# A fused encoder layer on one core: value projections first from unscaled x, weight sums one up turn earlier, two down steps prepared

## The reference, cut to what matters

```python
h = rms_norm(x, norm_mix)                       # x: (512 tokens, 1024)
q_a, k_a, v_a, q_b, k_b, v_b, u_c, g = split(h @ w_in)
o_a = chunked_rel_attention(q_a, k_a, v_a, q_norm_a, k_norm_a, rel_bias_a)   # 8 heads x 64
o_b = stick_breaking_attention(q_b, k_b, v_b)                                # 8 heads x 64
o_c = multiscale_pool(u_c, w_pool, pool_scale)
merged = sig(g0) * (o_a @ w_branch_a) + sig(g1) * (o_b @ w_branch_b) + sig(g2) * (o_c @ w_branch_c)
x = x + merged @ w_out
h2 = rms_norm(x, norm_ffn)
x = x + (silu(conv(h2 @ w_up_gate)) * conv(h2 @ w_up_value)) @ w_down        # conv of width 3 over tokens
```

## Time and profile before

| what | value |
|---|---|
| median of 3 runs | 835.34 us (834.24 to 835.59) |
| profiled execution, its own time | 834.84 us |
| its span in the trace | 832.7 us |
| PE busy | 815.1 us, 98% of the span |
| DVE busy | 601.5 us, 72% |
| ACT busy | 402.6 us, 48% |
| DMA | 113.25 MB, mean 136 GB/s |

### The profile page before, as it was taken

How to read it: one execution, slowest core, us unless ns; L and a number is a source line. 1 busy time by engine, 2 the same in 40 slices (tenths; PEclk the granted TensorE clock), 3 DMA queues, 4 the chain that set the end, 5 groups by cost and what they waited for, 6 DMA issues and landing times.

```text
span 832.7 us, 11778 instructions
## 1 busy us (share of the span) xinstructions
PE 815.1 (98%) x3855; PEld 677.1 (81%) x3855; DVE 601.5 (72%) x847; ACT 402.6 (48%) x560; POOL 102.1 (12%) x87
## 2 busy tenths in 40 slices
PE   5999999999999999999999999999999999899998
PEld 4888888888888888888888887888888888688886
DVE  5535888867678676555552579888778789998798
ACT  6434776665546544434341463433333334455653
POOL 2100010000000060000000013332232333300000
PEclk9999999999999999999999999999999999999999
DMA  6333242222222222333363326666556655666455
GB/s 207 103 102 89 66 124 77 79 74 66 86 76 66 74 77 88 93 98 100 89 214 104 129 72 202 203 202 201 189 191 199 196 191 185 218 210 191 149 186 177
DMA packets 129964, 113.25 MB, mean 136 GB/s; under 512 B 6052, under 2 KB 109192, under 8 KB 128528
## 3 DMA queue, kind: packets, MB, share of 16 engines
q1 hardware_dynamic: 129264, 110.77, 42.6%
q0 software_dynamic: 672, 2.12, 0.9%
HBM read 99.21 MB, written 13.65 MB: 136 GB/s over the span
## 4 chain that ended last, share of the span: by engine, by line
PE 93%; DVE 4%; ACT 1%; DMA 1%; issue 1%; SPq 0%; DVEq 0%; ACTq 0%
PE ps L1422 29%; PE ps L1423 28%; PE ps L1424 28%; PE ps L1516 2%; PE ps L1506 2%; PE ps L1531 1%; PE ps L1530 1%; DVE w_lo L872 1%; DMA x_in<-in_x_dram 1%; DVE conv_out L1259 1%; DVE out_sb L1412 0%; DVE conv_out L1262 0%; PE ps L1447 0%; DVE conv_in L1268 0%; ACT w_hi L497 0%
## 5 line engine op out<-in xcount | busy, mean ns | idle before, releaser
L1422 PE MATMUL ps<-h_lo,w_hi 128*128 128x512 f32 x704 | 276.9, 393 | 1.5 <-DVE h_lo L897 0.9
L1423 PE MATMUL ps<-h_hi,w_hi 128*128 128x512 f32 x704 | 274.2, 389 | 0.0
L1424 PE MATMUL ps<-h_hi,w_lo 128*128 128x512 f32 x704 | 274.1, 389 | 0.0
L872 DVE TENSOR_TENSOR w_lo<-w_raw,w_hi 128x1024 fp32r<-128x1024 f32 x119 | 149.8, 1259 | 137.3 <-ACT w_hi L503 77.9
L503 ACT ACTIVATE w_hi<-w_raw 128x1024 fp32r<-128x1024 f32 x97 | 102.8, 1060 | 191.9 <-PE ps L1424 183.4
L1422 PEld LDWEIGHTS ps<-h_lo,w_hi 128*128 128x128 f32 x704 | 132.2, 188 | 29.8 <-issue 1.6
L1424 PEld LDWEIGHTS ps<-h_hi,w_lo 128*128 128x128 f32 x704 | 132.2, 188 | 27.6
L1423 PEld LDWEIGHTS ps<-h_hi,w_hi 128*128 128x128 f32 x704 | 132.2, 188 | 26.5
L481 POOL TENSOR_TENSOR sg<-sg,conv_out 128x512 f32<-128x512 f32 x22 | 37.4, 1700 | 319.2 <-ACT sg L801 319.2
L1262 DVE SCALAR_TENSOR_TENSOR conv_out<-conv_in,par,conv_out 128x512 f32<-128x512 f32 x44 | 50.2, 1141 | 5.5 <-DVE conv_out L1259 0.2
L497 ACT ACTIVATE w_hi<-w_raw 128x1024 fp32r<-128x1024 f32 x23 | 24.4, 1059 | 53.3 <-PE ps L1424 53.2
(11 more groups left out here) (219 smaller groups left out, 1304.7 us busy)
## 6 DMA issues: line engine op xcount, KB each, us to landing
w_raw<-in_w_in_dram SPq DMA_DIRECT2D x104, 256.0 KB, 3.1
w_raw<-in_w_up_dram SPq DMA_DIRECT2D x88, 256.0 KB, 3.2
raw_t<-in_w_down_dram SPq DMA_DIRECT2D x11, 1024.0 KB, 9.1
down_sums<-t_sum SPq DMA_DIRECT2D x11, 1024.0 KB, 5.6
w_raw<-in_w_down_dram SPq DMA_DIRECT2D x33, 256.0 KB, 3.0
w_raw<-down_sums SPq DMA_DIRECT2D x33, 256.0 KB, 3.8
w_raw<-in_w_out_dram SPq DMA_DIRECT2D x16, 256.0 KB, 2.9
w_raw<-down_sums SPq DMA_DIRECT2D x22, 128.0 KB, 2.9
```

Source lines behind the costliest of these rows:

```text
L872: v.tensor_tensor(w_lo[:, slot, :], w_raw[:, slot, :], r32(w_hi[:, slot, :]), ALU.subtract)\
L1422: mm3(dst, l_hi, r_lo, start=start, stop=False, **kw)
L1423: mm3(dst, l_hi, r_hi, start=False, stop=False, **kw)
L1424: return mm3(dst, l_lo, r_hi, start=False, stop=stop, **kw)
```

## The change

Six edits.

1. **Start.** PE transposes x itself, without waiting for r. ACT and DVE split the transposed x (`xt_hi`, `xt_lo`), and the value units of branch A are computed from it first. The gain of norm_mix is multiplied into the value weights (`values_hi`, `values_lo`, the latter two operations of 128x512). r per token is multiplied into the values as they leave PSUM. Meanwhile h is made: DVE adds the parts back (`parts_added`), PE spreads r over a bank with two matmuls (`d_r_hi`, `d_r_lo`), DVE multiplies (`h_sum`), and both engines split again. The order of units becomes four of v_a, one of v_b, q and k of the first heads, and the other three of v_b. Only the first value unit is computed token block by token block.
2. 24 matmuls of 128x128 on constants (`WARM`) stand ahead of everything on PE. SP issues the first value unit after the first block of x. `g_row` is loaded from ACT's queue, and POOL no longer splits a weight unit.
3. **Weight sums.** Pairs 0 and 1 are summed during the w_out stage (after `lo` of its units 3 and 5), pair p in up turn p-1 after that; the last turn has none.
4. **Two steps.** `s_x` and `a_lo_x` of step 1 now stand ahead of the last up turn as well, and behind it only the two weight units of step 1 follow.
5. **Seam.** The last block of `x1` is added in two halves, with its own waits; the order of the transposes is adapted; in the first up turn a split moves ahead of a pair of taps and `spread_r` moves before the end of the second tile.
6. **Last bank.** The last output block is added in two halves of 128x256, stored by SP and by ACT.

```diff
@@ start, ACT
+            xt_split_hi(0)
+            values_hi(N_VA, 0)
+            for t in range(1, TT):
+                xt_split_hi(t)
+            values_hi(N_VA + 1, 1)
+            square(0)
+            square(1)
+            values_hi(N_VA + 2, 2)
...
+            hi(N_QK0 + 1, 0)
+            proj_a(0, 0, QK0_BANK, N_QK0 + 1, False)
+            values_hi(N_VB + 1, 1)
+            proj_a(1, 1, QK0_BANK + 1, N_QK0 + 2, False)
+            values_hi(N_VB + 2, 2)
+            norms_a(0, SS0_BANK)
+            values_hi(N_VB + 3, 3)
+            hat_hi(0, 0)
+            hat_hi(1, 1)
@@ start, SP
+            x_load(0)
+            values(N_VA, 0, V_A * P)
+            for t in range(1, TT):
+                x_load(t)
+            values(N_VA + 1, 1, V_A * P)
+            values(N_VA + 2, 2, V_A * P)
@@ start, PE
+            pe.wait_ge(heads_step, 2)
+            for _ in range(WARM):
+                mm3(ps[:, 2, 0:P], ones_heads[:, :], ones_heads[:, :], start=True, stop=True)
...
+            for t in range(3):
+                x_transposes(t)
+            pe.wait_ge(lo_ready, N_VA + 1)
+            for t in range(TT):
+                pe.wait_ge(xt_lo_ready, t + 1)
+                for kk in range(2):
+                    last = value_product(V_A_BANKS[t], kk, t, slice(kk * WB, kk * WB + WB), 0)
+                if t == 0:
+                    x_transposes(3)
...
+            values(N_VB + 1, V_B_BANKS, 1)
+            sumsq(0, 0, SS0_BANK)
+            sumsq(1, 1, SS0_BANK + 1)
+            values(N_VB + 2, V_B_BANKS, 2)
+            values(N_VB + 3, V_B_BANKS, 3)
@@ w_out stage, DVE
             for u in range(2, KD):
                 lo(N_OUT + u, u % 2)
+                if u in (3, 5):
+                    sums_first((u - 3) // 2)
+                    sums_second((u - 3) // 2)
@@ up, DVE
+                        if isinstance(jj, int) and jj == NP - 1:
+                            continue
                         if (i, gv) == (0, 1):
-                            sums_first(jj)
+                            sums_first(jj + 1)
                         if (i, gv) == (1, 0):
-                            sums_second(jj)
+                            sums_second(jj + 1)
@@ up_first, DVE
-                sums_first(0)
-                sums_second(0)
@@ last up turn, DVE
-            s_x(0, 0)
-            a_lo_x(0, 0)
+            for step in range(2):
+                s_x(step, step)
+                a_lo_x(step, step)
             up(KF // 2 - 1)
-            prepare_x(1, 1)
+            for u in range(2):
+                down_lo(2 + u, 1, u)
@@ end
-            for i, (b8, bank) in enumerate(((0, 4), (2, 5), (1, 6), (3, 7), (4, 0), (6, 1))):
+            for i, (b8, bank) in enumerate(((0, 4), (2, 5), (1, 6), (3, 7), (4, 0))):
...
+            d.wait_ge(bank_done, 6)
+            for q in range(2):
+                o = slice(q * HT, q * HT + HT)
+                v.tensor_tensor(out_sb[:, 6, o], ps[:, 1, o], x1[:, 3, o], ALU.add).then_inc(out_ready, 1)
```

More of the change, by code:

```diff
@@ L41 @@
 Q_A, K_A, V_A, Q_B, K_B, V_B, U_C, GATE = 0, 4, 8, 12, 16, 20, 24, 28
-N_QK0 = 0
-N_VA = 2
+N_VA = 0
+N_VB0 = 4
+N_QK0 = 5
 N_VB = 6
@@ L515, in _, with xt_split_hi, values_hi @@
[L515 to L521, removed]
+            def xt_split_hi(t):
+                a.wait_ge(xt_done, t + 1)
+                act(xt_hi[:, :, t * P:t * P + P], x_turned(t), ACT.Copy).then_inc(xt_hi_ready, 1)
+            def values_hi(n, u):
+                a.wait_ge(w_landed[u % 2], (n // 2 + 1) * 32)
+                if n == 0:
+                    a.wait_ge(gmix_ready, 1)
+                if n >= 2:
+                    a.wait_ge(unit_done, n - 1)
+                for i in range(2):
+                    c = slice(i * WB, i * WB + WB)
+                    last = act(w_hi[:, u % 2, c], w_raw[:, u % 2, c], ACT.Copy, scale=g_mix[:, 2 * u + i:2 * u + i + 1])
+                last.then_inc(hi_ready, 1)
@@ L523, in after, with h_split_hi @@
+            def h_split_hi(k):
+                a.wait_ge(h_sum_ready, k + 2)
+                act(h_hi[:, k:k + 2, :], h_sum[:, k:k + 2, :], ACT.Copy).then_inc(h_hi_ready, 2)
+            h_split_hi(0)
+            h_split_hi(2)
+            hi(N_QK0, 1)
+            for t in range(TT):
+                last = act(v_a[:, t, :], ps[:, V_A_BANKS[t], :], ACT.Copy, scale=tok[:, 5, t:t + 1])
+            last.then_inc(v_stored, 1)
+            h_split_hi(4)
+            h_split_hi(6)
             def after(n):
@@ L792, in up @@
                             down_hi(gv, 0, gv, 0)
-                        elif not (first and e == 0):
+                        elif not (first and e in (0, 2)):
                             hi_at(n + gv + 2, gv, jj * 2 + (N_UP // 2 + i + 1))
@@ new lines, in values_lo @@
+            def values_lo(n, u):
+                d.wait_ge(hi_ready, n + 1)
+                for i in range(2):
+                    c = slice(i * WB, i * WB + WB)
+                    last = v.scalar_tensor_tensor(out=w_lo[:, u % 2, c], in0=w_raw[:, u % 2, c],
+                                                  scalar=g_mix[:, 2 * u + i:2 * u + i + 1], in1=r32(w_hi[:, u % 2, c]),
+                                                  op0=ALU.mult, op1=ALU.subtract)
+                last.then_inc(lo_ready, 1)
@@ new lines, in parts_added @@
+            def parts_added(k):
+                v.tensor_tensor(h_sum[:, k:k + 2, :], r32(xt_hi[:, k:k + 2, :]), r32(xt_lo[:, k:k + 2, :]), ALU.add)\
+                    .then_inc(h_sum_step, 1)
+            d.wait_ge(gmix_ready, 1)
+            xt_split_lo(0)
+            values_lo(N_VA, 0)
+            for t in range(1, TT):
+                xt_split_lo(t)
+            values_lo(N_VA + 1, 1)
+            d.wait_ge(xt_lo_ready, TT)
+            parts_added(0)
+            values_lo(N_VA + 2, 2)
```

326 lines of the change are left out of this document (191 added, 135 removed).

## The result

| what | before | after |
|---|---|---|
| median of 13 runs, same chip | 835.24 us (834.13 to 836.24; one run took 1029.7) | 837.2 us (837.0 to 838.55) |
| ratio | | 1.003, 95% interval 1.0023 to 1.0037 |
| profiled execution, its own time | 834.84 us | 838.45 us |
| its span | 832.7 us | 836.8 us |
| PE busy | 815.1 us | 822.7 us (98%) |

The change makes the kernel slower by 2.0 us. My range ended at 837.2; the likeliest case, "same", was wrong, and what happened is rival (b).

A forecast was written before the change was run, and what follows sets the result against it. PE was taken as the bound, fed except in a few waits, so late units cost their lateness. Terms -2.2 +3.6 +1.7 -0.5 +2.9 -3.5 -1.7 -0.1 gave +0.2: 835.0 us, range 832.5 to 837.2.

The forecast's parts named there:

- "same": Whole kernel: no clear change, neither under 833.7 us nor over 837.0; chance 0.55.
- rival (b): Pauses at the last v_b unit and last up turn's third tile both cost the clock: +1.9, 836.9 us; chance 0.14.
- start, first unit done: Kernel start: the first value unit finishes earlier because PE needs no r, -2.2 us net.
- pause behind `sumsq`: Before the last v_b unit: PE waits for its weight split, queued behind the norms, +3.6 us.
- clock behind it: Slow products after a pause: +1.7 us behind `sumsq`, 0 behind the third tile of turn 10.
- sums out of turn 0: Up turn 1: the late unit at 511.59 goes once the weight sums leave turn 0, -0.5 us.
- pause at the third tile of turn 10: Last up turn: step 1's preparation stands ahead of the third tile's weight split, so PE waits, +2.9 us.
- wait at step 1: Seam into the down steps: step 1's activations are ready earlier, so PE's wait shrinks, -3.5 us.
- slow products there: Start of step 1: with a pause of only 0.5 us the clock does not fall, -1.7 us.
- step 2: Down steps: DVE's preparation for step 2 is ready at 729.4 against 730.2, so covered, 0 us.
- end: Last output bank: adding and storing it in halves saves only what half a transfer is shorter, -0.1 us.
- Rival (c): One charged stall is absent because ACT runs earlier or DVE's operations overlap: 831.5 us; chance 0.08.

The follow-up runs named there:

- e4: The changed kernel with twelve unused matmuls on PE before the last v_b unit, filling the pause behind `sumsq`: 835.6 us.
- e12: The changed kernel with twelve unused matmuls in each of two pauses, before the last v_b unit and before the last up turn's third tile: 834.04 us.
- e2: The changed kernel with step 1's preparation moved from ahead of the last up turn to inside that turn, behind its taps: 832.35 us.
- e13: The changed kernel with eight unused matmuls on PE before the last v_b unit: 835.73 us.
- e3: The changed kernel with the last v_b unit split ahead of the norms and step 1 prepared inside the last up turn: 827.99 us.
- e1: The changed kernel with the last v_b unit's weight split moved ahead of the norms on ACT and DVE: 832.93 us.
- e8: The changed kernel with the last v_b unit split before the norms, DVE's v_b copy before the next split, step 1 prepared behind the last up turn: 833.87 us.

## Why the prediction was wrong, step by step

| term | forecast | measured |
|---|---|---|
| start, first unit done | -2.2 | -2.45 (done at 19.38 for 22.29, and 0.45 for r) |
| pause behind `sumsq` | +3.6 | +3.6 from start to start (3.41 idle) |
| clock behind it | +1.7 | +1.6 in the median (e4), +2.95 in the profile |
| wait for `v_b` before the scores | 0 | +0.2 |
| sums out of turn 0 | -0.5 | -0.6 (+4.2 at the first up product, +3.6 at turn 10) |
| pause at the third tile of turn 10 | +2.9 | +3.3 |
| clock behind it | 0 | **+1.6** (e12, and in the profile) |
| wait at step 1 | -3.5 | -3.5 |
| slow products there | -1.7 | -1.7 |
| step 2 | 0 | +0.35 |
| end | -0.1 | +0.2 in the profile |
| sum | +0.2 | +2.6, where the medians differ by 2.0 |

The measured terms are read in spans. The changed kernel's profiled execution took 1.65 us more than its span and the earlier one 2.1, which is most of the 0.6 that the sum has too much.

**The step that failed** is the sentence "Here I take no fall of the clock (the pause is a microsecond shorter than the one in the rows)". I had one pause of 3.96 us with a fall and none without, so there was no row that bounded the clock's price from the other side, and still I put 0.4 on the forecast and 0.14 on rival (b). The runs show falls behind 3.97, 3.41, 3.16, 2.44 and 2.28 us; 1.60, 1.50, 0.69 and 0.44 us were passed at full pace in their profiles. So behind the 3.16 us at the third tile of turn 10 the forecast had 0 where eight slow products cost 1.6, which is three quarters of the miss of 2.2. The Trainium skill (TensorE: Matmul & The Clock Gate, "Why this matters for your kernels") warns of idle gaps over a length that it gives; the pause of 2.28 us is shorter than that and cost the clock in its profile, so here the measurement decides.

**Right, and in place:** both pauses, their releasers (`w_lo` L971 and L950), the missing wait near 511, the first product (12.9 for 13.1), and the seam, where the wait is 0.49 us and PEclk 1.00. Rival (c) is out, (d) too. Rival (b) is right in kind; its 836.9 was added up 0.2 too high (834.84 + 1.9 is 836.7).

**Right by luck.** The first product came when forecast, but not for the reason given: PE was held by the warming matmuls and then by `xt_lo`, not by the landing of block 1. And +1.7 for the clock behind the first pause agrees with the median only: in single profiles six products were slow or 14.

**Terms mis-sized.** The second pause: 3.3 for 2.9. The five operations took 3.13 us (709.56 to 712.69), 0.19 more went by before the first of them could start, and the slack that I took as 0.15 was nothing (before, the split ended at 707.56 and PE began the tile at 707.61, when it was due). Step 2: I called it covered; one `h_lo` takes 2.3 us instead of 1.2 beside POOL's product (DVE's two in 3.44 us), so `a_lo` of step 2 ends at 738.97, where PE would have started step 2 at 738.77, and step 2 follows step 1 by 5.78 us instead of 5.44. The end: two stores of 128x256 land 2.3 us after issue, no sooner than one of 128x512 (2.2), and the second is issued as late as the whole one was. The warming: "the 24 warming ones run before block 0 has landed" was wrong by 2.5 us, and cost nothing in the sum, because I had PE wait for block 1 until 9.25 anyway.

**Three things of 1.3 to 1.7 us that vary between executions** overlie these terms, and each is a stretch of slow clock: behind the first pause (six slow products in e2's profile, 14 in the changed kernel's), behind the second (eight in the changed kernel's profile, 13 in e13's), and at the start. In e3's profile the products at the start were slow until 15.9 and the scores 1.5 us later than in e1's, with the same instructions. (That start is read from the pace, 0.43 us a product; PEclk prints 1.00 there.) So a single profile of such a kernel is good for its ledger of places, not for tenths of its total.

## What to carry to other kernels

In this kernel a pause of PE cost its length and then, by the medians, some 1.6 us of slow products. From a row of one long pause you can't tell what a shorter one costs. Here 2.28 us cost the clock and 1.60 us did not, so count every pause from about 2 us on with its clock until a row shows otherwise. Before work is prepared earlier on DVE, ask which weight split it is put ahead of: here the same five operations cost 4.85 us ahead of the turn and nothing between its taps. The time in which an engine waits for a result (DVE idle 4.35 us ahead of `newton`) is where the next unit's split belongs. Edits that each look like half a microsecond can be the room that a larger one needs: the sums alone are worth 0.6 us, and with step 1 inside the turn 5.1, of which 3.5 are seen as waits.

## What the runs showed of the hardware

- Twelve useless matmuls in a pause of 3.4 us made the kernel 1.6 us faster (837.2 to 835.6), and two such sets 3.2 us (834.04).
- The fall comes at once behind some pauses (69.31, behind 2.28 us) and 1.5 us after the restart behind others (714.56 and 716.14, behind 3.16 us). The length of the pause doesn't decide which: behind 3.96 us it came at once in the kernel before (728.24) and 1.5 us late behind 3.97 us in e8. By its mean clock of 1.000, one execution in 12 of e1 had no fall.
- DVE and POOL hold each other up. In the changed kernel the tap of L1411 took 1.67 us at 730.47, while POOL's product of L512 ran, for a usual 0.75; POOL's product of L515 took 2.09 us at 732.33, beside DVE's `h_lo`, for 1.29 at 705.42.

```profile
729.82 1.77 POOL L512 TENSOR_TENSOR sg<-sg,conv_out 128x512 f32<-128x512 f32 x1 [8.30 <-ACT sg L875]
...
729.69 0.74 DVE L1408 SCALAR_TENSOR_TENSOR conv_out<-conv_in,par,conv_out 128x512 f32<-128x512 f32 x1
730.47 1.67 DVE L1411 SCALAR_TENSOR_TENSOR conv_out<-conv_in,par,conv_out 128x512 f32<-128x512 f32 x1
```

  The Trainium skill (SBUF — State Buffer, "SBUF: two separate sides") says that a DVE operation with two inputs in SBUF waits until GpSimd's instruction ends, if that one reads SBUF and started first. The trace agrees within 0.2 us: POOL's ends at 731.59, and DVE's 0.55 us later, where one alone takes 0.75.
